# Activation-table choice, a residual added by matmul, and per-tile normalisation in a two-block transformer kernel

## Chip, cores and metric

The kernel runs on one core of one Trainium2 chip. The metric is device time of one launch in microseconds (us), the median of the runs shown. Everything is float32 at the interface; the input has 256 tokens of width 1024, handled as two tiles of 128 tokens.

## What is computed

The reference chains two blocks. Cut to what matters here:

```python
# first block: attention, then a mixture of 32 experts, top 4
h = layer_norm(DEEPNORM_ALPHA * x + moba_attention(x, ...), ln_g[0], ln_b[0])   # ALPHA = 2 ** 0.25
f = moe_ffn(h, ...)
x = layer_norm(DEEPNORM_ALPHA * h + f, ln_g[1], ln_b[1])

# second block
h = rmsnorm(x, pre_mix_g);  z = h @ w_in                 # 1024 -> 3584
mix = concat(hgrn2_mixer(z...), gate_b * causal_dwconv(gate_c * conv_h)) @ w_out
x = x + rmsnorm(mix, post_mix_g)
h = rmsnorm(x, pre_ffn_g);  u = causal_dwconv(h @ ffn_w_up)   # 1024 -> 2 * 2816
y = (silu(gate) * val) @ ffn_w_down
out = x + rmsnorm(y, post_ffn_g)
```

Each normalisation needs one 1/sqrt per token. The forget gate of `hgrn2_mixer` needs exp, log(1 + exp) and exp again.

## The kernel before

Five engine programs are written out by hand, tied by counting semaphores; there is no scheduler. Instructions of an engine run in the order of the source, and `link(...)` makes an engine wait for its own last instruction.

- **First block.** The attention projections, attention, the first layer norm (`layer_norm`, L1311, with `h1` as its result), the router. Then 32 experts in turn (L705 to L798): TensorE does `gather`, `gate_up` (L668), `down_e` (L676) and `scatter` (L688), which adds an expert's output into the PSUM banks 4 to 7. The banks begin with the gated down biases (L729, at expert 1). SyncE streams each expert's weights in six pieces of 2 MB through a ring of nine slots, each load waiting until the piece nine places back has been used.
- **Second layer norm (L1471).** For each tile of 128 tokens VectorE adds `ALPHA * h1` to the banks (L1317, two halves of 512), takes the moments (`bn_stats` L1320, `bn_aggr` L1322), and then in `scale` applies them in two passes over 1024 columns (L1327, L1328), giving `x2`.
- **Roots.** 1/sqrt is made in two steps. VectorE writes the variance plus epsilon (`root_of`, L1294). ScalarE makes a rough root as exp(-0.5 * ln v) (`rough_root`, L952 and L953). VectorE refines it by one Newton step of four tiny instructions (`refine`, L1301 to L1304). There are 13 such roots, six in the two layer norms and the norm before the first product, one for the heads, six later.
- **Before each product of the second block.** ScalarE squares a tile of tokens and sums it (L1086, L1173), a root is made, VectorE scales the tile into `xn` (L1477, L1621). TensorE transposes `xn` (`turn_tokens`, L806), all of it after both tiles are ready. ScalarE evicts each of the eight transposed chunks of 128 channels rounded to the high part `x_hi` (`evict_hi`, L975), VectorE the remainder `x_lo` (`evict_lo`, L1238). `product` (L532) multiplies one piece of 256 weight columns: for each half of it and each of eight chunks, three matmuls of 128x256 (hi*hi, lo*hi, hi*lo), 48 in all. It begins after all eight chunks of both parts.
- **Weight pieces.** `split_hi` (ScalarE, L968, 128x2048) and `split_lo` (VectorE, L1231) make the two parts of a weight piece in two alternating buffers. The split of a piece waits for the product two places before it.
- **Forget gate (L1091 to L1103, L1486 to L1513).** After products 0 and 1 ScalarE does Abs, Exp, Ln on each half, VectorE turns them into log f, runs two prefix sums (L1497, L1499), the first decays, and only then `split_lo` of piece 4.
- **Third and fourth junction.** After the output projection (`mix`, L883) the squares of `mix` for both tiles, then two roots, `rms_residual` for both tiles (L1604 to L1611, giving `x3`), the squares of `x3` for both, two roots, `xn`, and the product with `ffn_w_up` (`UP`, 22 pieces). After the down projection (L924) squares of both tiles, two roots, `rms_residual` into `y_out`, and one store per tile.

## Time and profile before

| | |
|---|---|
| time before, median of 3 runs | 1524.03 us (1523.1 to 1526.42) |
| the profiled execution's own time | 1528.25 us |
| its span, first to last instruction | 1526.3 us |
| mean granted TensorE clock | 0.954 of full |
| busy in the span: TensorE matmul | 1359.2 us (89%) |
| VectorE / ScalarE / GpSimd | 431.0 / 361.1 / 57.6 us |
| moved by DMA | 482.57 MB, mean 316 GB/s |

Busy time says how long an engine worked, not whether anybody waited for it. The stretches are: attention up to about 175 us; the experts up to about 1100 us, in which the DMA engines move some 430 GB/s; the second block's mixer up to 1291 us; its feed-forward part to the end. TensorE is busy nearly throughout, so its idle stretches are what the other engines add.

### The profile page before, as it was taken

The page shows a single profiled execution, that of the slowest core. Times are in us where ns is not written, and L with a number is a line of the kernel's source. Part 1 is how long each engine was busy: PE and PEld are TensorE (multiplying, and loading weights), DVE is VectorE, ACT ScalarE, POOL GpSimd, SP SyncE. Part 2 cuts the span into 40 slices and gives each one's busy share as a digit, 9 for nine tenths or more (in the row PEclk, how much of TensorE's full clock was granted, in tenths as well). Part 3 has the DMA queues.
Part 4 walks back from the last instruction along what each step waited for, and adds up shares of the span by engine and source line. Part 5 has one row for each costly group of instructions (what it writes and reads, how often), then busy time and mean ns, then how long its engine had stood idle before and what let it go on. Part 6 is the DMA issues. An engine that isn't in the chain of part 4 may idle for free.

```text
span 1526.3 us, 16757 instructions
## 1 busy us (share of the span) xinstructions
PE 1359.2 (89%) x7266; PEld 723.4 (47%) x7266; DVE 431.0 (28%) x722; ACT 361.1 (24%) x559; POOL 57.6 (4%) x72
## 2 busy tenths in 40 slices
PE   6988799999969999999999999999748877599995
PEld 6964433333323333333333233333248873599984
DVE  3421321011011101011010010011255661577754
ACT  3332101011001101011010011011255423666644
POOL 1001000000000000000000000000000000033300
PEclk9999699999989999999999999999969999699998
DMA  9661498999999999999999999999933412255420
GB/s 379 272 262 49 171 431 346 431 429 430 432 429 428 432 430 430 431 430 431 429 432 432 430 430 431 430 431 429 418 120 129 148 56 84 82 175 203 176 83 27
DMA packets 73864, 482.57 MB, mean 316 GB/s; under 512 B 4316, under 2 KB 26896, under 8 KB 49216
## 3 DMA queue, kind: packets, MB, share of 16 engines
q1 hardware_dynamic: 71824, 475.53, 75.0%
q0 software_dynamic: 1968, 5.97, 1.3%
q8 instruction: 58, 0.95, 0.2%
q14 instruction: 14, 0.11, 0.0%
HBM read 480.42 MB, written 1.06 MB: 315 GB/s over the span
## 4 chain that ended last, share of the span: by engine, by line
PE 67%; DMA 19%; DVE 7%; ACT 4%; issue 2%; POOL 0%; SPq 0%; ACTq 0%; DVEq 0%
PE bank L668 20%; PE bank L542 16%; DMA ring<-in_moe_w_gate_up 15%; PE bank L676 11%; PE bank L924 4%; PE bank L641 3%; PE bank L522 3%; PE bank L688 3%; DMA ring<-in_w_in 3%; PE bank L883 2%; PE bank L610 2%; PE bank L660 2%; ACT w_hi L968 1%; DMA arena<-rel_rows 1%; DVE w_lo L1231 1%
## 5 line engine op out<-in xcount | busy, mean ns | idle before, releaser
L668 PE MATMUL bank<-ring,arena 128*64 128x512 f32 x2048 | 451.6, 595 | 21.0 <-DMA ring<-in_moe_w_gate_up 21.0
L668 PEld LDWEIGHTS bank<-ring,arena 128*64 128x64 f32 x2048 | 142.2, 137 | 328.2 <-issue 282.7
L676 PE MATMUL bank<-ring,arena 128*64 128x512 f32 x1024 | 226.8, 595 | 0.9 <-ACT arena L1044 0.9
L1429 DVE TENSOR_SCALAR arena<-bank 128x512 f32<-128x512 f32 x32 | 22.1, 692 | 674.9 <-PE bank L668 674.8
L542 PE MATMUL bank<-x_hi,w_hi 128*128 128x256 f32 x640 | 185.4, 290 | 9.9 <-DVE w_lo L1231 6.0
L542 PE MATMUL bank<-x_lo,w_hi 128*128 128x256 f32 x640 | 184.2, 288 | 0.0
L542 PE MATMUL bank<-x_hi,w_lo 128*128 128x256 f32 x640 | 184.0, 288 | 0.0
L1231 DVE TENSOR_TENSOR w_lo<-ring,w_hi 128x2048 fp32r<-128x2048 f32 x59 | 135.1, 2292 | 133.8 <-ACT w_hi L968 133.8
L968 ACT CAST w_hi<-ring 128x2048 fp32r<-128x2048 f32 x59 | 112.2, 1905 | 175.2 <-PE bank L542 142.7
L1038 ACT ACTIVATE arena<-arena 128x512 f32<-128x512 f32 x32 | 20.2, 630 | 508.3 <-DVE arena L1429 508.3
L676 PEld LDWEIGHTS bank<-ring,arena 128*64 128x64 f32 x1024 | 70.7, 137 | 135.7 <-issue 127.9
L542 PEld LDWEIGHTS bank<-x_hi,w_hi 128*128 128x128 f32 x640 | 125.9, 197 | 11.0 <-issue 8.7
L522 PE MATMUL bank<-cst,arena 128*128 128x128 f32 (+1 forms) x412 | 67.2, 314 | 69.6 <-DVE arena L1621 22.6
L542 PEld LDWEIGHTS bank<-x_lo,w_hi 128*128 128x128 f32 x640 | 125.7, 196 | 0.0
L542 PEld LDWEIGHTS bank<-x_hi,w_lo 128*128 128x128 f32 x640 | 125.6, 196 | 0.0
L522 PEld LDWEIGHTS bank<-cst,arena 128*128 128x128 f32 (+1 forms) x412 | 54.9, 197 | 103.0 <-DVE arena L1437 28.0
L641 PE MATMUL bank<-arena 128*64 128x512 f32 x256 | 65.7, 637 | 11.5 <-issue 10.5
L688 PE MATMUL bank<-arena 64*128 64x512 f32 x256 | 64.5, 622 | 4.8 <-ACT arena L1054 4.8
L1054 ACT COPY arena<-bank 128x512 f32<-128x512 f32 x32 | 18.8, 586 | 199.6 <-PE bank L676 199.6
L1648 DVE SCALAR_TENSOR_TENSOR ring<-ring,vcol 128x256 f32<-128x256 f32 x88 | 48.8, 594 | 0.8
L688 PEld LDWEIGHTS bank<-arena 64*128 64x128 f32 x256 | 22.2, 188 | 46.7 <-issue 40.2
L641 PEld LDWEIGHTS bank<-arena 128*64 128x64 f32 x256 | 19.0, 144 | 50.8 <-issue 49.7
(244 smaller groups left out, 1121.6 us busy)
## 6 DMA issues: line engine op xcount, KB each, us to landing
ring<-in_moe_w_gate_up SPq DMA_DIRECT2D x128, 2048.0 KB, 24.1
ring<-in_moe_w_down SPq DMA_DIRECT2D x64, 2048.0 KB, 26.0
ring<-in_ffn_w_up SPq DMA_DIRECT2D x22, 1024.0 KB, 7.4
ring<-in_w_in SPq DMA_DIRECT2D x7, 2048.0 KB, 19.5
ring<-in_a_w_in SPq DMA_DIRECT2D x6, 2048.0 KB, 18.8
ring<-in_ffn_w_down SPq DMA_DIRECT2D x5, 2048.0 KB, 7.7
ring<-in_a_w_out SPq DMA_DIRECT2D x2, 2048.0 KB, 17.5
ring<-in_w_out SPq DMA_DIRECT2D x2, 2048.0 KB, 8.2
```

Source lines behind the costliest of these rows:

```text
L522: return pe.transpose(dst, src, ident[0:rows, 0:rows])
L542: last = mm(dst[:, j * T:(j + 1) * T], lhs, rhs, start=c == 0 and n == 0, stop=c == KC - 1 and n == 2)
L610: last = mm(bank[2 * g + t][:, :], oT[:, h, t * P:(t + 1) * P], slot(ATTN_OUT[g], KC)[:, h, :], start=h == 0, stop=h == H - 1)
L641: last = mm(bank[2][half * 64:half * 64 + 64, :], sel[:, t, :], h1[:, t, half * 512:(half + 1) * 512], start=t == 0, stop=t == NT - 1)
L660: mm(bank[q][half * 64:half * 64 + 64, :], bias_sel[rows, :], bgu[rows, half, :], start=True, stop=False)
L668: last = mm(bank[q // 2][half * 64:half * 64 + 64, :], chunk(xeT, c), w[:, c % 2, q * 512:(q + 1) * 512], start=False, stop=c == KC - 1)
L676: last = mm(bank[3][half * 64:half * 64 + 64, :], chunk(actT, c), w[:, c % 4, half * 512:(half + 1) * 512], start=c == 0, stop=c == KC - 1)
L688: last = mm(bank[4 + 2 * half + t][:, :], selgT[rows, t, :], y_item[rows, :], start=False, stop=True, skip_group_check=True)
L924: last = mm(bank[2 * t + g][:, :], a, w[:, cols], start=c == 0 and k == 0, stop=c == FB - 1 and k == 2)
L968: copy(like(w_hi, p), pieces[p][2]).then_inc(hi_ready, 1)
L1231: tt(like(w_lo, p), pieces[p][2], like(w_hi, p).bitcast(f32), ALU.subtract).then_inc(lo_ready, 1)
L1648: last = stt(y[:, g, :], u[:, g, j:j + T], vcol[:, col:col + 1], y[:, g, :], ALU.mult, ALU.add)
```

## The change

Line numbers of the changed file differ. The change does four things.

1. **One activation table.** Four places of ScalarE's program call for the table set that has both logarithm and exponential (at the start, after the experts, before the first `decay`, before the squares at the end), so that Ln and Exp alternate without a load between them.
2. **Second residual by TensorE.** At expert 24, after the scatter of expert 23, four matmuls of 128x512 add `ALPHA * I` times `h1` to the banks 4 to 7. VectorE makes `alpha_i` at expert 1. The second layer norm then reads the banks directly: `bn_stats` from PSUM, first pass of the scale from PSUM in two halves, no separate addition.
3. **Tile by tile.** At each of the three later junctions squares, root, scaling and the next squares are ordered for tile 0 first and then tile 1, and TensorE transposes tile 0 as soon as its `xn` is ready.
4. **Chunk by chunk.** The first product after a transposition (`IN2` piece 0, `UP` piece 0) waits before each chunk in its first half for that chunk alone.

```diff
+RESIDUAL_AT = 24
+        alpha_i = at(7168, P)
...
-            def product(p, dst, tokens_stationary=False):
+            def product(p, dst, tokens_stationary=False, fresh=0):
...
                     for c in range(KC):
+                        if fresh and j == 0:
+                            pe.wait_ge(hT_hi, fresh * KC - KC + c + 1)
+                            pe.wait_ge(hT_lo, fresh * KC - KC + c + 1)
...
+                if i == RESIDUAL_AT:
+
+                    pe.wait_ge(alpha_ready, 1)
+                    for g in range(2):
+                        for t in range(NT):
+                            mm(bank[4 + 2 * g + t][:, :], alpha_i, h1[:, t, g * 512:(g + 1) * 512], start=False, stop=True,
+                               skip_group_check=True)
...
             def turn_tokens(src, ready, ps):
 
-                for t in range(NT):
-                    pe.wait_ge(*ready(t))
+                def half(b, j, t):
+                    return turn(bank[b][:, j * T + t * P:j * T + (t + 1) * P],
+                                src[:, t, (2 * b + j) * P:(2 * b + j + 1) * P])
+
+                pe.wait_ge(*ready(0))
                 for b in range(4):
                     for j in range(2):
-                        for t in range(NT):
-                            last = turn(bank[b][:, j * T + t * P:j * T + (t + 1) * P],
-                                        src[:, t, (2 * b + j) * P:(2 * b + j + 1) * P])
-                    last.then_inc(ps, 1)
+                        half(b, j, 0)
+                pe.wait_ge(*ready(1))
+                for b in range(4):
+                    half(b, 0, 1)
+                    half(b, 1, 1).then_inc(ps, 1)
...
-            pe.wait_ge(hT_hi, KC)
-            pe.wait_ge(hT_lo, KC)
             for r in range(8):
-                for last in product(IN2 + r, bank[r], r >= 4):
+                if r < 4:
+                    pe.wait_ge(hT_lo, min(KC, 2 * r + 2))
+                for last in product(IN2 + r, bank[r], r >= 4, fresh=r == 0):
...
-            pe.wait_ge(x3_ready, NT)
...
-                for last in product(UP + f, bank[4 + f % 2]):
+                for last in product(UP + f, bank[4 + f % 2], fresh=2 * (f == 0)):
...
+            log_exp = "natural_log_exp_and_others"
+            nc.scalar.preload_act_table_set(log_exp)
...
+            nc.scalar.preload_act_table_set(log_exp)
             rough_root(2)
             rough_root(3)
             for t in range(NT):
                 act.wait_ge(x2_ready, t + 1)
                 activate(squares_at(t * D, D), x2[:, t, :], ACT.Square, accum_out=ss[:, t:t + 1]).then_inc(x_sq, 1)
-            rough_root(4)
-            rough_root(5)
+                rough_root(4 + t)
...
+            for t in range(NT):
+                act.wait_ge(mix_ps, 2 * t + 2)
+                squares_of(t, (2 + 2 * t, 3 + 2 * t), mix_sq)
+                rough_root(7 + 2 * t)
                 act.wait_ge(x3_ready, t + 1)
-                activate(squares_at(t * D, D), x3[:, t, :], ACT.Square, accum_out=ss2[:, 4 + t:5 + t]).then_inc(x_sq, 1)
-            rough_root(9)
-            rough_root(10)
+                activate(squares_at(2 * D + t * D, D), x3[:, t, :], ACT.Square, accum_out=ss2[:, 4 + t:5 + t]).then_inc(x_sq, 1)
+                rough_root(8 + 2 * t)
...
+            nc.scalar.preload_act_table_set(log_exp)
+            for t in range(NT):
+                act.wait_ge(down_ps, t + 1)
+                squares_of(t, (2 * t, 2 * t + 1), down_sq)
+                rough_root(11 + t)
...
+                    ts(alpha_i, ident, ALPHA, None, ALU.mult).then_inc(alpha_ready, 1)
...
-            layer_norm(x2, h1, bank[4:8], 2, lambda t: (moe_done, t + 1), x2_ready)
+            for t in range(NT):
+                dve.wait_ge(moe_done, t + 1)
+                for g in range(2):
+                    last = dve.bn_stats(stats[:, t, g, :], bank[4 + 2 * g + t][:, :])
+                link(last)
+                link(dve.bn_aggr(moments[:, t, :], stats[:, t, :, :].rearrange("p a b -> p (a b)")))
+                root_of(2 + t, moments[:, t, 1:2], 1.0, LN_EPS)
+            for t in range(NT):
+                r = refine(2 + t)
+                for g in range(2):
+                    cols = slice(g * 512, (g + 1) * 512)
+                    last = stt(x2[:, t, cols], bank[4 + 2 * g + t][:, :], moments[:, t, 0:1], row_g[:, cols],
+                               ALU.subtract, ALU.mult)
+                link(last)
+                if t:
+                    dve.wait_ge(x_sq, 1)
+                    root_of(4, ss[:, 0:1], 1.0 / D, RMS_EPS)
+                stt(x2[:, t, :], x2[:, t, :], r, row_b, ALU.mult, ALU.add).then_inc(x2_ready, 1)
+            for t in range(NT):
+                if t:
+                    dve.wait_ge(x_sq, 2)
+                    root_of(5, ss[:, 1:2], 1.0 / D, RMS_EPS)
+                r = refine(4 + t)
                 ts(xn[:, t, :], x2[:, t, :], r, None, ALU.mult).then_inc(xn_ready, 1)
```

**Order, place one.** ScalarE from the end of expert 31 to the first eviction of `x_hi`. Before (L1054 copies the last expert's output out of PSUM, L952/L953 are Ln/Exp of a root, L1086 the squares):

```order
269 L1054 COPY arena<-bank 128x512
270 L952 ACT_TABLE_LOAD
271 L952 ACTIVATE arena<-arena 128x1
272 L953 ACT_TABLE_LOAD
273 L953 ACTIVATE arena<-arena 128x1
...
278 L1086 ACTIVATE arena<-arena 128x1024 x2
279 L952 ACT_TABLE_LOAD
280 L952 ACTIVATE arena<-arena 128x1
281 L953 ACT_TABLE_LOAD
282 L953 ACTIVATE arena<-arena 128x1
```

And in the changed program (L1070 the copy, L968/L969 the root, L1103 the squares):

```order
265 L1070 COPY arena<-bank 128x512
266 L1098 ACT_TABLE_LOAD
267 L968 ACTIVATE arena<-arena 128x1
268 L969 ACTIVATE arena<-arena 128x1
269 L968 ACTIVATE arena<-arena 128x1
270 L969 ACTIVATE arena<-arena 128x1
271 L1103 ACTIVATE arena<-arena 128x1024
272 L968 ACTIVATE arena<-arena 128x1
273 L969 ACTIVATE arena<-arena 128x1
274 L1103 ACTIVATE arena<-arena 128x1024
```

One load stands where eight stood, and the first root of the norm has moved between the two squares. In the whole program of ScalarE there are 7 table loads where there were 35.

**Order, place two.** VectorE in the second layer norm, with what each row waits for. Before, tile 1's moments and the first scale:

```order
400 L1317 SCALAR_TENSOR_TENSOR arena<-arena,bank 128x512 [waits moe_done]
401 L1317 SCALAR_TENSOR_TENSOR arena<-arena,bank 128x512
402 L1320 BN_STATS arena<-arena 128x6 [waits dve_step]
403 L1320 BN_STATS arena<-arena 128x6
404 L1322 BN_AGGR arena<-arena 128x2 [waits dve_step]
...
410 L1327 SCALAR_TENSOR_TENSOR arena<-arena 128x1024 [waits dve_step]
411 L1328 SCALAR_TENSOR_TENSOR arena<-arena 128x1024 [waits dve_step]
```

In the changed program tile 1's moments and its scale:

```order
399 L1490 BN_STATS arena<-bank 128x6 [waits moe_done]
400 L1490 BN_STATS arena<-bank 128x6
401 L1492 BN_AGGR arena<-arena 128x2 [waits dve_step]
...
414 L1498 SCALAR_TENSOR_TENSOR arena<-bank,arena 128x512 [waits dve_step]
415 L1498 SCALAR_TENSOR_TENSOR arena<-bank,arena 128x512
416 L1309 TENSOR_SCALAR arena<-arena 128x1 [waits x_sq,dve_step]
417 L1504 SCALAR_TENSOR_TENSOR arena<-arena 128x1024
```

The addition is gone, the moments and the first pass read PSUM, and the variance of the next root (L1309, `root_of`) is written ahead of tile 1's last pass.

## Rows read from the trace of the kernel before

**Rows 1.** Waits of TensorE from 1120 to 1330 us: us in total, times, longest.
```profile
PE bank L522 <- DVE arena L1621: 22.6, 1, 22.6
PE bank L522 <- DVE arena L1477: 21.3, 1, 21.3
...
PE bank L542 <- DVE w_lo L1231: 4.6, 1, 4.6
```
**Rows 2.** Groups of instructions of ScalarE: count, busy us, mean ns, idle before.
```profile
L952 ACT ACT_TABLE_LOAD x13 | 16.7, 1283 | 0.2
```
**Rows 3.** Timeline of VectorE, 1102 to 1124 us: start, us, instruction, [idle before].
```profile
1102.96 1.28 DVE L1317 SCALAR_TENSOR_TENSOR arena<-arena,bank 128x512 f32<-128x512 f32 x2
1104.27 1.29 DVE L1320 BATCH_NORM_STATS2 arena<-arena 128x6 f32<-128x512 f32 x2
...
1109.61 1.28 DVE L1327 SCALAR_TENSOR_TENSOR arena<-arena 128x1024 f32<-128x1024 f32 x1
...
1119.75 0.16 DVE L1301 TENSOR_TENSOR arena<-arena 128x1 f32<-128x1 f32 x1 [4.18 <-ACT arena L953]
...
1123.12 0.16 DVE L1301 TENSOR_TENSOR arena<-arena 128x1 f32<-128x1 f32 x1 [1.78 <-ACT arena L953]
...
1123.90 0.75 DVE L1477 TENSOR_SCALAR arena<-arena 128x1024 f32<-128x1024 f32 x1
```
**Rows 4.** Timelines of ScalarE, VectorE and TensorE, 1124 to 1137 us.
```profile
1125.92 3.40 ACT L975 ACTIVATE x_hi<-bank,vcol 128x256 fp32r<-128x256 f32 x8 [2.83 <-PE bank L522]
...
1126.79 3.44 DVE L1238 SCALAR_TENSOR_TENSOR x_lo<-bank,vcol,x_hi 128x256 fp32r<-128x256 f32 x8 [2.14 <-ACT x_hi L975]
...
1124.80 3.65 PE L522 MATMUL bank<-cst,arena 128*128 128x128 f32 x16 [21.29 <-DVE arena L1477]
1130.33 0.55 PE L542 MATMUL bank<-x_hi,w_hi 128*128 128x256 f32 x1 [1.89 <-ACT x_hi L975]
...
1136.33 0.28 PE L542 MATMUL bank<-x_lo,w_hi 128*128 128x256 f32 x1
```
**Rows 5.** Timeline of VectorE, 1150 to 1161 us.
```profile
1151.06 0.69 DVE L1490 SCALAR_TENSOR_TENSOR arena<-bank,ring 128x512 f32<-128x512 f32 x1 [2.09 <-ACT ring L1098]
...
1158.38 2.29 DVE L1231 TENSOR_TENSOR w_lo<-ring,w_hi 128x2048 fp32r<-128x2048 f32 x1
```
**Rows 6.** Timelines of ScalarE and VectorE, 1295 to 1319 us.
```profile
1300.55 1.04 ACT L1173 ACTIVATE arena<-arena 128x1024 f32<-128x1024 f32 x1
1301.49 0.19 ACT L1173 ACTIVATION_READ_ACCUMULATOR arena<-arena 128x1 f32 x1
...
1295.19 0.16 DVE L1301 TENSOR_TENSOR arena<-arena 128x1 f32<-128x1 f32 x1 [9.48 <-ACT arena L953]
...
1295.97 1.41 DVE L1608 SCALAR_TENSOR_TENSOR arena<-bank,arena 128x512 f32<-128x512 f32 x2
1297.41 1.22 DVE L1611 TENSOR_TENSOR arena<-arena 128x1024 f32<-128x1024 f32 x1
...
1313.52 2.29 DVE L1231 TENSOR_TENSOR w_lo<-ring,w_hi 128x2048 fp32r<-128x2048 f32 x1 [0.26 <-ACT w_hi L968]
1315.73 3.22 DVE L1238 SCALAR_TENSOR_TENSOR x_lo<-bank,vcol,x_hi 128x256 fp32r<-128x256 f32 x8
```
**Rows 7.** Chain that ended last, in order of time: the whole product with `ffn_w_up`.
```profile
1319.05 128.44 PE bank L542 x1056
```
**Rows 8.** Timeline of VectorE from 1508 us to the end.
```profile
1514.34 0.16 DVE L1301 TENSOR_TENSOR arena<-arena 128x1 f32<-128x1 f32 x1 [5.34 <-ACT arena L953]
...
1522.04 1.23 DVE L1611 TENSOR_TENSOR arena<-arena 128x1024 f32<-128x1024 f32 x1
```
**Rows 9.** Page, costliest groups: `gate_up` of all experts, with its idle time and releaser.
```profile
L668 PE MATMUL bank<-ring,arena 128*64 128x512 f32 x2048 | 451.6, 595 | 21.0 <-DMA ring<-in_moe_w_gate_up 21.0
```
**Rows 10.** Timeline of TensorE, attention's output projection, 32 matmuls of 128x512.
```profile
122.94 27.73 PE L610 MATMUL bank<-ring,arena 128*128 128x512 f32 x64 [0.46 <-ACT arena L1016]
```
**Rows 11.** DMA issues: size and us from issue to landing.
```profile
ring<-in_moe_w_gate_up SPq DMA_DIRECT2D x128, 2048.0 KB, 24.1
```

More of the change, by code:

```diff
@@ L265, in build @@
         xe_ps, xe_ready, xeT_ps, xeT_ready = sem("xe_ps"), sem("xe_ready"), sem("xeT_ps"), sem("xeT_ready")
+        alpha_ready = sem("alpha_ready")
         sel_ready, selg_ready, bsel_ready = sem("sel_ready"), sem("selg_ready"), sem("bsel_ready")
@@ L1159, in _, with squares_of @@
                              scale=vcol[:, 160 + h:161 + h]).then_inc(mT_ready, 1)
-            def squares_of(ps, count, banks, done):
-                for n, b in enumerate(banks):
-                    if n % count == 0:
-                        act.wait_ge(ps[0], ps[1](n))
-                    last = activate(squares_at(n * 512, 512), bank[b][:, :], ACT.Square, accum_out=ss2[:, n:n + 1])
-                    last.then_inc(done, 1)
-            squares_of((mix_ps, lambda n: n + 2), 2, (2, 3, 4, 5), mix_sq)
-            rough_root(7)
-            rough_root(8)
+            def squares_of(t, banks, done):
+                for g, b in enumerate(banks):
+                    n = 2 * t + g
+                    activate(squares_at(n * 512, 512), bank[b][:, :], ACT.Square, accum_out=ss2[:, n:n + 1]).then_inc(done, 1)
             for t in range(NT):
+                act.wait_ge(mix_ps, 2 * t + 2)
+                squares_of(t, (2 + 2 * t, 3 + 2 * t), mix_sq)
+                rough_root(7 + 2 * t)
                 act.wait_ge(x3_ready, t + 1)
-                activate(squares_at(t * D, D), x3[:, t, :], ACT.Square, accum_out=ss2[:, 4 + t:5 + t]).then_inc(x_sq, 1)
-            rough_root(9)
-            rough_root(10)
+                activate(squares_at(2 * D + t * D, D), x3[:, t, :], ACT.Square, accum_out=ss2[:, 4 + t:5 + t]).then_inc(x_sq, 1)
+                rough_root(8 + 2 * t)
             split_hi(UP)
@@ L1214, in _ @@
                 split_a_hi(p)
-            act.wait_ge(down_ps, 1)
-            squares_of((down_ps, lambda n: n // 2 + 1), 2, (0, 1, 2, 3), down_sq)
-            rough_root(11)
-            rough_root(12)
+            nc.scalar.preload_act_table_set(log_exp)
+            for t in range(NT):
+                act.wait_ge(down_ps, t + 1)
+                squares_of(t, (2 * t, 2 * t + 1), down_sq)
+                rough_root(11 + t)
         @block.vector
@@ L1470, in _ @@
             dve.wait_ge(ln1_in, 32)
-            layer_norm(x2, h1, bank[4:8], 2, lambda t: (moe_done, t + 1), x2_ready)
             for t in range(NT):
-                dve.wait_ge(x_sq, t + 1)
-                r = root(4 + t, ss[:, t:t + 1], 1.0 / D, RMS_EPS)
+                dve.wait_ge(moe_done, t + 1)
[20 more added lines that the diff above has]
+                r = refine(4 + t)
                 ts(xn[:, t, :], x2[:, t, :], r, None, ALU.mult).then_inc(xn_ready, 1)
@@ L1615, in _ @@
                 dve.wait_ge(mix_sq, 2 * t + 2)
-                rms_residual(7 + t, t, (ss2[:, 2 * t:2 * t + 1], ss2[:, 2 * t + 1:2 * t + 2]), (2 + 2 * t, 3 + 2 * t), post_g, x2, x3,
-                             x3_ready)
-            for t in range(NT):
+                rms_residual(7 + 2 * t, t, (ss2[:, 2 * t:2 * t + 1], ss2[:, 2 * t + 1:2 * t + 2]), (2 + 2 * t, 3 + 2 * t), post_g,
+                             x2, x3, x3_ready)
                 dve.wait_ge(x_sq, NT + t + 1)
-                r = root(9 + t, ss2[:, 4 + t:5 + t], 1.0 / D, RMS_EPS)
+                r = root(8 + 2 * t, ss2[:, 4 + t:5 + t], 1.0 / D, RMS_EPS)
                 ts(xn[:, t, :], x3[:, t, :], r, None, ALU.mult).then_inc(xn_ready, 1)
```

2 lines of the change are left out of this document (removed).

## Prediction

> **What bounds the kernel now.** I read the page first, then the waits of TensorE, then the timelines at each wait. TensorE is busy for most of the span, and in the experts it waits for weights only. So time can be saved where TensorE stands still for other engines. Its waits in the second block [rows 1] name two such places: 21.3 us before the transposes of `x2` and 22.6 us before those of `x3`. A third, 4.6 us, is before weight piece 4. A fourth is no wait of TensorE: after its last matmul only squares, roots, `rms_residual` and stores are left [rows 8].
>
> What fills those waits is a chain between VectorE and ScalarE. A table load takes 1283 ns [rows 2]. The reader is to see in [rows 3] that VectorE idles 1.78 us for a rough root when one load lies between Ln and Exp. That idle time is 0.50 without it: 1.78 - 1.28. The refinement that follows takes 0.78 (1123.12 to 1123.90).
>
> **First junction, experts to product 0.** The sum starts at 1102.96, when VectorE takes up the norm; the weight splits ahead of it are not moved.
> - Norm before: from 1102.96 to 1109.61 it did two tiles' moments and one refinement. So a tile took (6.65 - 0.78) / 2 = 2.93, of which 1.31 is the addition (1102.96 to 1104.27) and 1.62 the moments. After: 2 x 1.62 gives 1106.2. The rough roots come 0.5 us after their variances and are hidden, since tile 1's moments lie between.
> - Scale of a tile after: 0.78, a first pass from PSUM in two halves, 1.44 as in [rows 6] (1295.97 to 1297.41), and a second of 1.28 [rows 3]. Tile 0 is ready at 1109.7, tile 1 at 1113.2. Tile 0's squares, root and Ln/Exp lie beside tile 1's passes.
> - `xn` of tile 0: 0.78 + 0.75, so 1114.7. Tile 1's squares (1.04 in the like row of [rows 6], about 1.2 with handing over) end at 1114.4, before that. Then epsilon 0.15, the 0.50, 0.78, 0.75: `xn` of tile 1 at about 1116.8. Before it was 1124.65. **7.9 us saved.**
> - Transposes: tile 0's eight take half of the 3.65 us [rows 4] and lie in the wait. Before, the first eviction began 1.12 us after the first transpose, after four of them; now two are needed, 0.46 us less. VectorE follows 0.87 us behind. Product 0 overwrites bank 0 and needs two chunks of `x_lo`, 2 x 0.43. So it starts 2.5 us after tile 1's transposes begin, where it took 5.53 (1124.80 to 1130.33). **3.0 us saved.** Later chunks come every 0.43 us, and three matmuls take 0.64 us at the low clock (28 starts from 1130.33 to 1136.33 are 0.214 each): no starving.
>
> **Forget gate.** Two loads on ScalarE lie between product 1 and the last Ln; VectorE takes it up at 1151.06 and, after prefix sums and decays, gets to the split of piece 4 at 1158.38 [rows 5]. TensorE waits 4.6 us for that split [rows 1], more than is saved: 2 x 1.28 = **2.6 us**. Next in line would be the end of product 3, 2 us further off. The load before the sigmoid stays.
>
> **Heads' root.** Its two loads go, but TensorE is in the 14 us of `mix` over the convolution half meanwhile: nothing.
>
> **Second junction, `mix` to `UP`.** Tile 0's rough root now comes before tile 1's squares: VectorE's idle 9.48 us [rows 6] shrinks to 0.50, so its refinement starts at 1286.2 instead of 1295.19. From there: 0.78 + 1.44 + 1.22 = 3.44 to `x3` of tile 0 at 1289.65; squares 1.2; epsilon and root 0.65; 0.78 and 0.75 for `xn`, 1293.0. Tile 1: adding two sums, epsilon and root 0.85, 3.44, squares 1.2, root 0.65: 1299.1. ScalarE's split of piece `UP` follows, 1.9 us, so VectorE's split starts at 1301.0 where it started at 1313.52. **12.5 us saved.** `x_lo` begins 2.21 after that as before, and the product needs one chunk, 0.43, instead of eight, 3.22: **2.8 us** more. Chunks come every 0.40 and three matmuls take 0.365 at the high clock (128.44 / 1056 = 0.122 each [rows 7]): 0.3 us lost. Together 15.0 us. The split of `UP + 1` ends some 6 us after the start, just in time.
>
> **End.** Tile 0's root no longer waits behind tile 1's squares and two loads: idle 5.34 [rows 8] becomes 0.50. Tile 1's idle 1.78 (the same 1.78 stands before four roots of a tile 1) becomes 0.50. The last addition at 1522.04 and the store follow. 4.84 + 1.28 = **6.1 us.**
>
> **Costs.** The four residual matmuls: the output projection did 32 of this shape in 27.73 us [rows 10], so 3.5 us. They are at expert 24, where TensorE waits for weights: it waits 21.0 us in all for them [rows 9], over the last dozen experts, and a load lands 24.1 us after issue though it moves 2 MB, under 5 us at 430 GB/s [rows 11]. So some four transfers are queued, and a place freed 3.5 us later starves nobody. I take 0, the bounds are 0 and 3.5. `alpha_i` on VectorE and the extra waits on ScalarE: 0, they lie beside `gate_up` of an expert.
>
> `bn_stats` from PSUM has no row. The nearest from below is 1.31 a pair from SBUF [rows 3]; from above, 1.44 for a pair that streams PSUM [rows 6]. I take the upper one: 2 x 0.13 = 0.25 us lost. The Trainium skill (Perfetto Trace Analysis, Optimizing Scalar/DVE Operations) gives VectorE an overhead of about 125 ns on PSUM against 60 on SBUF; by this, as an estimate, the four would lose 0.26.
>
> TensorE's clock: it fell during the idle wait and rose at 1136, 11 us after the first transpose, 6 after product 0 began [rows 4]. I assume the same, with 0.7 us lost because tile 0's transposes now stand apart. Bounds: no matmul at the low clock gains 28 x 0.092 = 2.6 at the first and about 1.5 at the second product, and both first products wholly at the low clock lose 5.
>
> **Sum.** 7.9 + 3.0 + 2.6 + 15.0 + 6.1 = 34.6, less 0.25 and 0.7: 33.7 us. The profiled execution took 1528.25 (span 1526.3), so its like would take 1494.6. It stands 4.2 above the median of the runs, 1524.03, from which I get **1490.3**. What a measurement of this kernel can tell from no change is about 0.2%, 3 us.
>
> **Rivals.**
> - *TensorE stays at 1.2 GHz after the split starts.* Transposes in two bursts and a product that waits chunk by chunk may not raise the clock. If it stays down for the first two products at both junctions, some 150 more matmuls cost 0.092: 14 us, so 1504. Against: at 1130.33 it began just as cold and was fast 6 us later [rows 4], and in the first junction the chunks come faster than it can use them. The Trainium skill (TensorE: Matmul & The Clock Gate, A second HAM failure mode: psum-queue depth-cycling) tells of short idling between groups of matmuls that makes the clock go up and down; by this rule it would come out as here, 1504. Chance 7%.
> - *The loads stay* or something else takes their time, that is, the change doesn't do what it says. Then each root on the path costs 1.3 to 2.6 more: 2.8 in the first junction, 6.5 in the second, 3.4 at the end, 2.6 in the forget gate, 15.3 in all. 1506. Against: the changed program has 7 loads, before 35. Chance 4%.
> - *The residual is paid:* the 3.5 us are on the path, 1494. For it: every expert after the pause waits for weights, so the stage ends with the DMA stream. Against: the queue depth above. Chance 5%.
> - *Slower than before.* If the clock fell at the new junction and did not come back within the `UP` product, all of its matmuls would pay 0.092. Beyond 33.7 / 0.092 = 366 of them, a third of the 1056, the gain is gone; all 1056 cost 97 us, so 1587. Against: within this product's 128.44 us there is hardly room for matmuls at 1.2 GHz. Chance 1%.
>
> **How the numbers follow.** My forecast has 83%. Its own range is from 34.6 + 4.1 saved, 1485, to the loss of 5 more on the clock and 3.5 for the residual, 1499. Two more for another chip and day: 1484 to 1500, which leaves out the rivals of 1504 and above. Faster 0.98, within 0.2% 0.01, slower 0.01.
>
> **What would show it.** Seven table loads. TensorE's wait before the first transposes of `x2` near 11 us with next to none before tile 1's; before those of `x3` near 2.3 us, and near 6 before tile 1's. No wait over 2.5 us for piece 4. VectorE idle 0.5 us before each refinement on the path. The tail from the last matmul to the last addition shorter by 6. Wrong: gate_up waits longer after expert 24; the first product's matmuls 0.21 us apart for much longer than 6 us; VectorE's idle before refinements still 1.8.

## The result and the profile after

The changed kernel takes **1487.31 us** (median, 1484.68 to 1490.52), the kernel before 1524.28 us (1523.1 to 1526.42) beside it. The ratio is 0.9757, 95% interval 0.9735 to 0.9779. Forecast were 1490.3 us and a range of 1484 to 1500. Measured once more later, both kernels anew, it was 1489.84 against 1523.86 us, ratio 0.9764 (0.9748 to 0.978). So 37.0 and 34.0 us were gained where 33.7 were forecast.

| | before | after |
|---|---|---|
| the profiled execution's own time, us | 1528.25 | 1487.63 |
| its span | 1526.3 | 1485.7 |
| mean granted TensorE clock | 0.954 | 0.966 |
| busy: TensorE matmul | 1359.2 | 1357.4 |
| VectorE / ScalarE / GpSimd | 431.0 / 361.1 / 57.6 | 428.5 / 324.3 / 57.9 |

The page of the changed kernel: busy time, then the group of `gate_up` (the line of [rows 9]).

```profile
PE 1357.4 (91%) x7274; PEld 720.5 (48%) x7274; DVE 428.5 (29%) x721; ACT 324.3 (22%) x531; POOL 57.9 (4%) x72
...
L674 PE MATMUL bank<-ring,arena 128*64 128x512 f32 x2048 | 451.1, 595 | 18.1 <-DMA ring<-in_moe_w_gate_up 18.0
```

TensorE is busy 1.8 us less, ScalarE 36.8 less. 28 loads of 1.283 us are 35.9, which is nearly all of the latter. The reader should not take 36.8 for the gain because it is near 37: many of those loads lay beside other work. What was gained shows in TensorE's waits.

Waits of TensorE in the changed kernel, 1060 to 1330 us (us in total, times, longest), the answer to [rows 1]:

```profile
PE bank L525 <- DVE arena L1510: 10.1, 1, 10.1
PE bank L525 <- DVE arena L1653: 8.2, 2, 6.0
...
PE bank L548 <- DVE w_lo L1246: 2.4, 1, 2.4
```

21.3 us became 10.1 (before `x2` is transposed), 22.6 became 8.2 in two pieces (before `x3` is), 4.6 became 2.4 (weight piece 4).

**First junction.** Timeline of VectorE, 1100 to 1114 us, the answer to [rows 3]:

```profile
1100.59 1.30 DVE L1490 BATCH_NORM_STATS2 arena<-bank 128x6 f32<-128x512 f32 x2
...
1103.88 0.15 DVE L1316 TENSOR_TENSOR arena<-arena 128x1 f32<-128x1 f32 x1
...
1104.64 1.41 DVE L1498 SCALAR_TENSOR_TENSOR arena<-bank,arena 128x512 f32<-128x512 f32 x2
...
1112.84 0.16 DVE L1316 TENSOR_TENSOR arena<-arena 128x1 f32<-128x1 f32 x1 [0.51 <-ACT arena L969]
...
1113.61 0.75 DVE L1510 TENSOR_SCALAR arena<-arena 128x1024 f32<-128x1024 f32 x1
```

Counted from the start of the norm, the first refinement comes after 3.29 us and `xn` of tile 1 is ready after 13.77 (1114.36 - 1100.59). Before it was ready after 21.69 (1124.65 - 1102.96). In the whole stretch VectorE idles once, 0.51 us for tile 1's rough root.

What follows on the three engines, the answer to [rows 4]:

```profile
1115.15 3.02 ACT L991 ACTIVATE x_hi<-bank,vcol 128x256 fp32r<-128x256 f32 x8 [2.34 <-PE bank L525]
...
1116.02 3.23 DVE L1253 SCALAR_TENSOR_TENSOR x_lo<-bank,vcol,x_hi 128x256 fp32r<-128x256 f32 x8 [1.65 <-ACT x_hi L991]
...
1112.33 4.07 PE L525 MATMUL bank<-cst,arena 128*128 128x128 f32 x16 [10.14 <-DVE arena L1510]
1116.95 0.58 PE L548 MATMUL bank<-x_hi,w_hi 128*128 128x256 f32 x1 [0.56 <-DVE x_lo L1253]
...
1120.53 0.39 PE L548 MATMUL bank<-x_lo,w_hi 128*128 128x256 f32 x1
...
1120.88 0.28 PE L548 MATMUL bank<-x_hi,w_hi 128*128 128x256 f32 x1
```

Product 0 starts at 1116.95, 0.93 us after the first `x_lo` begins: two chunks of it are done and six are still to come (the row of all eight lasts 3.23 us). It then never waits for a chunk. Its matmuls start 0.21 us apart until 1120.7 and 0.12 apart afterwards.

**Forget gate and piece 4.** Timeline of VectorE, the answer to [rows 5]:

```profile
1132.42 2.29 DVE L1246 TENSOR_TENSOR w_lo<-ring,w_hi 128x2048 fp32r<-128x2048 f32 x1 [2.08 <-ACT w_hi L984]
1134.63 0.68 DVE L1523 SCALAR_TENSOR_TENSOR arena<-bank,ring 128x512 f32<-128x512 f32 x1
...
1141.96 2.29 DVE L1246 TENSOR_TENSOR w_lo<-ring,w_hi 128x2048 fp32r<-128x2048 f32 x1
```

Before, L1490 (now L1523) had waited 2.09 us for the logarithm. Now it has no idle time at all in front: it follows the split of piece 3, which ends at 1134.7, 0.5 us after ScalarE's last Ln (1134.2).

**Second junction.** Timelines of VectorE and TensorE in the changed kernel, the answer to [rows 6]:

```profile
1267.08 0.16 DVE L1316 TENSOR_TENSOR arena<-arena 128x1 f32<-128x1 f32 x1 [0.50 <-ACT arena L969]
...
1280.00 0.16 DVE L1316 TENSOR_TENSOR arena<-arena 128x1 f32<-128x1 f32 x1 [0.50 <-ACT arena L969]
...
1281.79 2.29 DVE L1246 TENSOR_TENSOR w_lo<-ring,w_hi 128x2048 fp32r<-128x2048 f32 x1 [0.27 <-ACT w_hi L984]
...
1273.98 1.65 PE L525 MATMUL bank<-cst,arena 128*128 128x128 f32 x8 [2.29 <-DVE arena L1653]
1281.58 1.97 PE L525 MATMUL bank<-cst,arena 128*128 128x128 f32 x8 [5.95 <-DVE arena L1653]
1284.62 0.55 PE L548 MATMUL bank<-x_hi,w_hi 128*128 128x256 f32 x1 [1.07 <-ACT x_hi L991]
```

The 9.48 us of [rows 6] before tile 0's refinement are 0.50. All four refinements have 0.50 or 0.51 in front.

**End.** Timeline of VectorE, the answer to [rows 8]:

```profile
1475.01 0.16 DVE L1316 TENSOR_TENSOR arena<-arena 128x1 f32<-128x1 f32 x1 [0.50 <-ACT arena L969]
...
1481.43 1.23 DVE L1644 TENSOR_TENSOR arena<-arena 128x1024 f32<-128x1024 f32 x1
```

**Chain of waits** (start, us, what), the long products:

```profile
1116.95 13.46 PE bank L548 x96
...
1144.30 36.32 PE bank L548 x288
...
1284.62 128.45 PE bank L548 x1056
```

The last is 128.44 in [rows 7]: the `UP` product pays nothing for a start chunk by chunk.

### The span in stages

Spans differ by several us for reasons that are not the change, so from here on stages are compared. Each step is the us from one mark to the next; "x96" are products 0 and 1, "x288" products 4 to 9. All are read from one profile per kernel.

| step | before | again | after | again |
|---|---|---|---|---|
| norm of `x2` begins | 1102.96 | 1099.58 | 1100.59 | 1099.18 |
| to product 0 | 27.37 | 27.37 | 16.36 | 16.35 |
| to product 4 | 30.39 | 27.83 | 27.35 | 27.56 |
| of this, x96 | 14.33 | 11.77 | 13.46 | 13.68 |
| to `mix`, convolution half | 100.01 | 99.35 | 97.29 | 98.83 |
| of this, x288 | 37.52 | 36.84 | 36.32 | 36.32 |
| to `mix`, second half | 16.10 | 17.79 | 16.10 | 17.79 |
| to `UP` product | 42.22 | 42.22 | 26.93 | 26.93 |
| to down product | 136.24 | 137.23 | 136.24 | 136.43 |
| to the last squares | 54.72 | 54.72 | 54.72 | 54.72 |
| to the end | 16.29 | 16.31 | 10.12 | 10.11 |

Three steps repeat to 0.02 us in both profiles of either kernel: 27.37 to 16.36 (11.0), 42.22 to 26.93 (15.3), 16.30 to 10.12 (6.2). Those are the change's. Between products 0 and 4, without x96, 16.06 became 13.88 (2.2). x288 is 0.5 to 1.2 less. Together 35.2 to 35.9 us. The rest wanders by itself: x96 between 11.8 and 14.3, the second half of `mix` at 16.10 or 17.79, the time of the norm's start.

### The profile page after: what moved, and what is told of

It is laid out like the page before. It is cut to its first block, busy times and chain, and to the rows that moved or that the text cites. A ratio compares the mean times of both kernels' runs of the same rounds, so it can differ in the third digit from the quotient of the medians.

```text
span 1485.7 us, 16760 instructions
## 1 busy us (share of the span) xinstructions
PE 1357.4 (91%) x7274; PEld 720.5 (48%) x7274; DVE 428.5 (29%) x721; ACT 324.3 (22%) x531; POOL 57.9 (4%) x72
## 4 chain that ended last, share of the span: by engine, by line
PE 68%; DMA 19%; DVE 8%; ACT 2%; issue 2%; POOL 0%; SPq 0%; ACTq 0%; DVEq 0%
PE bank L674 21%; PE bank L548 16%; DMA ring<-in_moe_w_gate_up 15%; PE bank L682 11%; PE bank L937 3%; PE bank L647 3%; PE bank L694 3%; PE bank L525 3%; DMA ring<-in_w_in 3%; PE bank L616 2%; PE bank L666 2%; PE bank L899 1%; DVE w_lo L1246 1%; ACT w_hi L984 1%; DMA arena<-rel_rows 1%
## 5 line engine op out<-in xcount | busy, mean ns | idle before, releaser
L674 PE MATMUL bank<-ring,arena 128*64 128x512 f32 x2048 | 451.1, 595 | 18.1 <-DMA ring<-in_moe_w_gate_up 18.0
L1054 ACT ACTIVATE arena<-arena 128x512 f32<-128x512 f32 x32 | 20.2, 630 | 505.0 <-DVE arena L1445 505.0
L525 PE MATMUL bank<-cst,arena 128*128 128x128 f32 (+1 forms) x412 | 66.8, 311 | 44.4 <-DVE arena L1510 10.1
L647 PE MATMUL bank<-arena 128*64 128x512 f32 x256 | 65.7, 637 | 11.5 <-issue 10.5
L1070 ACT COPY arena<-bank 128x512 f32<-128x512 f32 x32 | 18.7, 585 | 199.6 <-PE bank L682 199.6
```

Source lines behind the costliest of these rows:

```text
L525: return pe.transpose(dst, src, ident[0:rows, 0:rows])
L647: last = mm(bank[2][half * 64:half * 64 + 64, :], sel[:, t, :], h1[:, t, half * 512:(half + 1) * 512], start=t == 0, stop=t == NT - 1)
L674: last = mm(bank[q // 2][half * 64:half * 64 + 64, :], chunk(xeT, c), w[:, c % 2, q * 512:(q + 1) * 512], start=False, stop=c == KC - 1)
```

## The experiments

Two explanations compete throughout: that the forecast's parts are right one by one, or that its sum is right by chance, with a part too large beside one too small. The runs undo or isolate one part each. Unless said otherwise a ratio is to the kernel before, and a diff is to the changed kernel.

### Both kernels again

> The kernel before, unchanged, for a second profile of it. In the first one the down-bias matmuls at expert 1 took 6.74 us and the norm started at 1103.0; in the changed kernel and all its variants they took 3.7 to 4.5 and it started at 1097 to 1101. If that is how TensorE's clock happened to stand, it differs here by 1 us or more; if the change caused it, both numbers come back. The two times differ by less than 2 us. After the 4.6 us wait for piece 4 the 288 matmuls take 37.5 us again, and not the 36.3 of the variants with the 2.4 us wait, if the length of a wait sets the clock behind it.

Measured: 1524.71 against 1523.86 us, ratio 1.0009 (1.0 to 1.0018). The second profile bears on the late start of the norm in the first profile of before. Chains of waits of the two executions of the same kernel, the gated down biases at expert 1, of the first:

```profile
224.32 6.74 PE bank L729 x8
```

and of the second, with its first long products:

```profile
224.35 4.09 PE bank L729 x8
...
1126.95 11.77 PE bank L542 x96
...
1154.78 36.84 PE bank L542 x288
```

The same eight matmuls, starting at the same time, took 6.74 or 4.09 us; from 224.3 to 231.1 the mean granted clock was 0.54 in the first execution and 0.75 in the second. So the 2.4 us by which the norm began earlier after the change are not the change's: the kernel before has its start at 1102.96 or 1099.58. One expectation was missed: x288 took 36.84 us and not 37.5 again, so its excess over the 36.3 behind the shorter wait is 0.5 to 1.2 us.

> The changed kernel, unchanged, for a second profile and a time on the same chip as the other two. The steps between marks of the program (norm to product 0 16.4, mix to UP 26.9, last squares to end 10.1) come back within 0.1; what differs lies in stretches where TensorE's clock moves.

Measured: 1489.84 us, ratio 0.9764 (0.9748 to 0.978). The stages are in the table above.

### The activation table alone

Diff to the kernel before, the added line at each of the four places:

```diff
+            nc.scalar.preload_act_table_set(log_exp)
```

> The kernel before with the table choice alone (four calls), everything else as before. Theory A (each load on a waiting path costs its 1.28 us and nothing else): 3.8 us before product 0, 2.2 at the forget gate (there VectorE's split of piece 3 takes over), 7.7 before UP, 3.8 at the end, together 17.5 us: about 1506.8. Rival B (the loads were mostly hidden and the reordering did the work): under 8 us, 1516 or more.

Measured: 1502.75 us, before 1524.95 beside it, ratio 0.9861 (0.9842 to 0.9881). That is 22.2 us. Waits of TensorE, 1060 to 1330 us:

```profile
PE bank L522 <- DVE arena L1483: 17.2, 1, 17.2
PE bank L522 <- DVE arena L1627: 14.6, 1, 14.6
...
PE bank L542 <- DVE w_lo L1237: 2.4, 1, 2.4
```

The wait for piece 4 is already down to 2.4: that part of the gain is the table's alone. Stages, against the second profile of before: 4.0 in the first junction (27.37 to 23.38), 2.2 to product 4 without x96, 0.6 in x288, 8.0 in the second junction (42.22 to 34.25), 4.0 at the end. Together 18.8, where 17.5 were expected; the other 3.4 us of the medians lie in no stage that repeats.

### All but the activation table

The line is taken out at all four places.

```diff
-            nc.scalar.preload_act_table_set(log_exp)
```

> The changed kernel without the four calls, so with 35 loads again. Theory A: roots cost 1.3 to 2.6 us more each on the path, 2.8 + 6.5 + 3.4, and 2.2 at the forget gate: 15 us above the changed kernel, about 1502. Rival B: within 5 us of the changed kernel. If the gain of the table alone and the loss without it differ by more than 3 us, the table and the reordering overlap.

Measured: 1510.26 us, ratio 0.9895 (0.9878 to 0.9911), a gain of 14.7. Without the table the change is worth 14.7, the table alone 22.2, together 36.9, where the whole gave 37.0. They add up. By stages the loads cost 3.1 in the first junction, 2.2 to product 4 without x96, 0.9 in x288, 8.75 in the second junction and 3.4 at the end: 18.3, near the 18.8 from the other side.

The second junction cost more than expected. ScalarE's timeline there, from the end of the squares of `x3`, tile 0, to the load before that root's Exp (L967 is Ln, L968 Exp):

```profile
1283.91 0.19 ACT L1185 ACTIVATION_READ_ACCUMULATOR arena<-arena 128x1 f32 x1
1284.11 1.28 ACT L967 ACT_TABLE_LOAD   x1
1285.40 0.20 ACT L967 ACTIVATE arena<-arena 128x1 f32<-128x1 f32 x1
1285.62 1.28 ACT L968 ACT_TABLE_LOAD   x1
```

The load for Ln starts when the squares have ended. VectorE needs some 0.2 us from there for the variance plus epsilon (0.5 after the squares of `mix`, where it first adds two sums), so only that much of the load is hidden. Of the 2.57 us of two loads 2.19 stand on the path of each root, the mean of the four (8.75 / 4). The forecast's rival "the loads stay" had 6.5 us for this stage.

### The residual on VectorE again

```diff
-                if i == RESIDUAL_AT:
+                if False:
...
+                    last = stt(x2[:, t, cols], h1[:, t, cols], ALPHA, bank[4 + 2 * g + t][:, :], ALU.mult, ALU.add)
...
-                    last = dve.bn_stats(stats[:, t, g, :], bank[4 + 2 * g + t][:, :])
+                    last = dve.bn_stats(stats[:, t, g, :], x2[:, t, g * 512:(g + 1) * 512])
```

> The changed kernel with the second residual added by VectorE as before and the norm's passes on SBUF; the tile order stays. Theory A: two additions of 1.31 us come back and two first passes shrink by 0.16: 2.3 us above the changed kernel, all of it between the start of the norm and product 0. Rival C (the matmuls at expert 24 delay the weight stream): it gains 3.5 there, so 1 us below the changed kernel or more, and the norm starts earlier.

Measured: 1492.37 us, ratio 0.9792 (0.9771 to 0.9813). The first junction is 18.72 instead of 16.36, so the residual on TensorE is worth 2.4 us there. The medians say 2.5 to 5, which the wandering of the other stages covers. Page of this kernel, `gate_up`:

```profile
L674 PE MATMUL bank<-ring,arena 128*64 128x512 f32 x2048 | 451.6, 595 | 20.8 <-DMA ring<-in_moe_w_gate_up 20.8
```

and the moments from SBUF in VectorE's timeline:

```profile
1100.57 1.29 DVE L1493 BATCH_NORM_STATS2 arena<-arena 128x6 f32<-128x512 f32 x2
```

This answers two costs at once. `gate_up` waits 20.8 us without the four matmuls and 18.1 with them: most of their 3.5 us displace a wait for weights. The norm starts at 1099.25 without them, and between 1097.11 and 1101.23 in the ten profiles with them. What stands in front of it in the chain of waits is a load of weights, after it their splits; here in the changed kernel:

```profile
1053.67 40.47 DMA ring<-in_w_in
```

And a pair of `bn_stats` takes 1.29 from SBUF, 1.30 from PSUM: the 0.25 us that I had taken for four are not there. The Trainium skill (Perfetto Trace Analysis, Optimizing Scalar/DVE Operations) has an overhead of about 125 ns on PSUM against 60 on SBUF; for this instruction the trace does not show it. The first pass of the scale is slower from PSUM, 1.41 for two halves against 1.28 for one whole pass from SBUF. Reading PSUM alone does not explain that: the addition of [rows 3] reads a bank too, as its second operand, and two halves of it take 1.28. What makes the difference was not isolated.

### The residual at expert 12

```diff
-RESIDUAL_AT = 24
+RESIDUAL_AT = 12
```

> The changed kernel with the four residual matmuls at expert 12, where TensorE does not wait for weights, instead of 24. If the weight stream sets the end of the experts, TensorE's 3.5 us at expert 12 are taken up by later waits for weights: 0 to 1 us, and the waits of gate_up shrink by about 3.5. If TensorE's own work sets it, 3.5 us above the changed kernel.

Measured: 1487.49 us, ratio 0.9768 (0.9749 to 0.9786): no difference. Page, `gate_up`:

```profile
L674 PE MATMUL bank<-ring,arena 128*64 128x512 f32 x2048 | 451.1, 595 | 18.2 <-DMA ring<-in_moe_w_gate_up 18.1
```

It waits as long as with the matmuls at expert 24. That they cost nothing is thus shown for both places. My reason for the place (they come when TensorE waits anyway) was not what mattered: it is enough that waits for weights still follow.

### No start chunk by chunk

```diff
+            pe.wait_ge(hT_hi, KC)
+            pe.wait_ge(hT_lo, KC)
             for r in range(8):
-                if r < 4:
-                    pe.wait_ge(hT_lo, min(KC, 2 * r + 2))
-                for last in product(IN2 + r, bank[r], r >= 4, fresh=r == 0):
+                for last in product(IN2 + r, bank[r], r >= 4):
```

and the same before the `UP` product.

> The changed kernel with both first products waiting for all eight chunks again. Theory A: six chunks of 0.40 to 0.43 us at the first, seven at the second less the 0.3 it was held up: 2.5 + 2.5, 5 us above the changed kernel. Rival D (a product that waits chunk by chunk runs longer on the low clock): only 2 to 3 us, since both products then run through faster once begun.

Measured: 1494.35 us, ratio 0.9801 (0.978 to 0.9821). First junction 18.75 (+2.4), second 29.62 (+2.7). The chain of waits at the first shows what comes back, eight evictions and a stretch in which nothing else is seen:

```profile
1112.39 3.04 ACT x_hi L993 x8
1115.43 1.16 issue
1116.58 14.05 PE bank L548 x96
```

The two steps are 5.1 us, expected were 5; medians differ by 7.0, or 4.5 against the later run of the changed kernel.

### Both tiles transposed together

```diff
-                pe.wait_ge(*ready(0))
+                for t in range(NT):
+                    pe.wait_ge(*ready(t))
                 for b in range(4):
                     for j in range(2):
-                        half(b, j, 0)
-                pe.wait_ge(*ready(1))
-                for b in range(4):
-                    half(b, 0, 1)
-                    half(b, 1, 1).then_inc(ps, 1)
+                        for t in range(NT):
+                            last = half(b, j, t)
+                    last.then_inc(ps, 1)
```

> The changed kernel with all transposes after both tiles, in the old order; chunks stay. Theory A: the first eviction waits for four transposes instead of two, 0.5 us at the first junction; nothing at the second, where VectorE's split of the weights is later. Together 0.5 us above. Theory E (the early burst of tile 0's transposes is what raised TensorE's clock earlier and gave the 3 us more than forecast): 2 to 4 us above, with a longer stretch at 1.2 GHz after the products start.

Measured: 1485.91 us, ratio 0.9742 (0.9726 to 0.9759). Nothing is lost, though the junctions grow by 0.9 and 0.7 us. The chain of waits at the first product,

```profile
1115.73 11.52 PE bank L548 x96
```

and at the `UP` product:

```profile
1283.62 127.78 PE bank L548 x1056
```

x96 is 11.52 where the changed kernel had 13.46, and x1056 is 0.67 less. 96 matmuls at 0.12 are 11.5, so product 0 began at the high clock, 2.4 GHz. Theory E, that tile 0's early burst raises the clock for the product, falls. That the two bursts lower it is not shown either: transposed apart, x96 was 11.79 and 11.80 in two of the other runs. One profile each cannot settle it, and it stays open whether the early transposes of tile 0 are worth anything.

### The old order of tiles from `mix` on

The squares of both tiles, then both roots, `rms_residual` of both, as before; likewise after the down projection.

```diff
             for t in range(NT):
                 act.wait_ge(mix_ps, 2 * t + 2)
                 squares_of(t, (2 + 2 * t, 3 + 2 * t), mix_sq)
-                rough_root(7 + 2 * t)
+            rough_root(7)
+            rough_root(8)
+            for t in range(NT):
                 act.wait_ge(x3_ready, t + 1)
```

> The changed kernel with squares and roots of the second junction and of the end in the order of before (both squares, both roots), table, residual and chunks as changed. Theory A: 4 us at the second junction and 2.3 at the end, 6 us above the changed kernel. Rival B (the reordering is the bulk): over 12 us.

Measured: 1493.63 us, ratio 0.9792 (0.9773 to 0.9812). Second junction 31.56 (+4.6), end 12.31 (+2.2); expected were 4 and 2.3. VectorE's timeline before the first refinement of `mix`:

```profile
1272.74 0.16 DVE L1320 TENSOR_TENSOR arena<-arena 128x1 f32<-128x1 f32 x1 [6.77 <-ACT arena L969]
```

6.77 us of idle time, where [rows 6] had 9.48 with the loads and the changed kernel has 0.50. So 2.71 of the 9.48 were loads, and 6.27 the order.

### A busy TensorE before the first product

Nine matmuls of 128x512 (two records each) whose result nobody uses are put ahead of the transposes of `x2`, where TensorE waits.

```diff
+            for _ in range(9):
+                mm(bank[0][:, :], ident, h1[:, 0, 0:512], start=True, stop=True)
             turn_tokens(xn, lambda t: (xn_ready, t + 1), hT_ps)
```

> The changed kernel with nine added matmuls of 128x512 (their result is not used) on TensorE right after the last scatter, in the 10.1 us in which it waits for xn of tile 0. If the low clock of product 0 comes from that wait, the clock is high when the transposes start: these take half as long and the first two products 11.5 to 12 us instead of 13.5, together 2 to 3 us below the changed kernel. If the added work overruns the wait or the clock falls anyway, 0 or above.

Measured: 1486.54 us, ratio 0.9768 (0.9751 to 0.9785). No gain can be told: 1487.49 us were measured beside it for the run with the residual at expert 12. Timeline of TensorE:

```profile
1100.95 8.69 PE L840 MATMUL bank<-arena,cst 128*128 128x512 f32 x18
1111.17 1.09 PE L525 MATMUL bank<-cst,arena 128*128 128x128 f32 x8 [1.53 <-DVE arena L1512]
1113.26 1.97 PE L525 MATMUL bank<-cst,arena 128*128 128x128 f32 x8 [1.00 <-DVE arena L1512]
```

and its windows (us, then busy us of TensorE, its weight loads, VectorE, ScalarE, GpSimd; granted clock; DMA share; GB/s):

```profile
1100.00:1110.00 10.00, 9.64 (x22) 3.69 (x18) 9.44 (x26) 2.65 (x9) 0.55 (x2) 0.88 0.99 387
1110.00:1117.00 7.00, 4.27 (x21) 3.63 (x22) 4.63 (x15) 4.29 (x12) 1.24 (x2) 0.69 0.68 266
```

Tile 0's eight transposes took 1.09 us, at a granted clock of 1.00; eight of the same shape take 1.65 in the changed kernel's second junction. But in the 7 us around the two bursts the mean clock was 0.69, tile 1's transposes took 1.97 again with the clock at 0.50, and x96 is 13.39 where it was 13.46. So in this execution the clock fell behind the filling, not in the long wait. TensorE was busy for 4.27 of the 7 us, 1.2 of them product 0 itself, with pauses of 1.53, 1.00 and 0.56. Neither the long wait nor the two short bursts decides alone how product 0 starts: in the runs with the residual at expert 12 and with the old order from `mix` on, the wait before the transposes is 10.6 and 10.5 us, the bursts stand apart in the same way, and product 0 begins at a clock of 1.00 (x96 11.79 and 11.80). What decides stays open.

### The split of piece 4 earlier

```diff
             link(dve.memset(marks[:, 64:HG * T:128], 1.0))
+            split_lo(IN2 + 4)
...
             decays(0)
-            split_lo(IN2 + 4)
```

That is ahead of the second prefix sum.

> The changed kernel with VectorE's split of piece 4 ahead of the second prefix sum, alone. TensorE's wait of 2.4 us goes. If it costs its length, products 0 to 9 take 2.4 us less than the changed kernel's 63.7; if it also pulls the clock down behind it, 4 us less, since all 288 matmuls behind it then run at the high clock. The time 2 to 4 us below the changed kernel.

Measured: 1485.36 us, ratio 0.9744 (0.9721 to 0.9766). The wait is gone, and products 0 to 9 are one piece of the chain:

```profile
1116.09 59.43 PE bank L548 x480
```

The changed kernel took 27.35 + 36.32 = 63.67 for them. A wait of 2.4 us was worth 4.2. Of the other 1.8 some 1.6 lie behind it: from the first to the last start of the 288 matmuls it is 36.02 us in the changed kernel and 34.44 here, and 34.44 again in the next run. Windows of 5.30 us right behind the wait, in the kernel before:

```profile
1160.70:1166.00 5.30, 5.28 (x24) 5.28 (x25) 3.37 (x3) 0.00 (x0) 0.00 (x0) 0.50 0.25 54
```

and in the changed kernel:

```profile
1144.30:1149.60 5.30, 5.30 (x32) 5.30 (x33) 3.34 (x3) 0.10 (x1) 0.00 (x0) 0.68 0.27 56
```

TensorE is full in both, yet does 24 matmuls behind the wait of 4.6 us, with the clock at 0.50 throughout, and 32 behind that of 2.4. In the second profile of before the clock came back earlier, with a mean of 0.57 over the same 5.30 us. That is the part of x288 that the change gained, and it repeats: x288 took 36.27 to 36.33 us in all nine profiles with the wait of 2.4, and 36.84, 37.19 and 37.52 in the three with that of 4.6.

### Splits earlier at both places

The same for piece 4, and the splits of pieces `UP` and `UP + 1` moved ahead of the squares of `mix`, on ScalarE and VectorE.

```diff
+            split_hi(UP)
+            split_hi(UP + 1)
             for t in range(NT):
                 act.wait_ge(mix_ps, 2 * t + 2)
                 squares_of(t, (2 + 2 * t, 3 + 2 * t), mix_sq)
```

> A version that may beat both: the changed kernel with the splits of UP pieces 0 and 1 moved ahead of the squares of mix (ScalarE and VectorE are idle during mix), and the split of piece 4 moved ahead of the second prefix sum. By the trace of the changed kernel the wait for piece 4 is 2.4 us and the first x_lo before UP waits 0.8 us for the split: 3 us below the changed kernel, about 1484. If another wait takes their place (the first decays come 2.3 us later), 0.8 or nothing.

Measured: **1483.68 us**, ratio 0.9721 (0.9701 to 0.9742), the fastest of all. Against the changed kernel it is 3.6 us by the medians; the intervals of the two ratios overlap a little, so the stages carry the claim. 59.49 for products 0 to 9 (the 4.2 of the run above), and the second junction is 26.10 instead of 26.93. At the second junction 0.8 were expected and 0.8 came, of 2.3 us of splits there (VectorE's 2.29 that ends at 1284.08 in the changed kernel): once the split is gone, the transposes and evictions are next.

## Why the prediction was right

Point by point, by its steps (us gained; measured is by stages):

| step | forecast | measured |
|---|---|---|
| first junction | 7.9 + 3.0 - 0.25 = 10.65 | 11.0 |
| forget gate | 2.6 | 2.2 |
| heads' root | 0 | 0 (16.10 or 17.79 in both kernels) |
| second junction | 12.5 + 2.8 - 0.3 = 15.0 | 15.3 |
| end | 6.1 | 6.2 |
| residual matmuls | 0 | 0 |
| clock | -0.7 | +0.5 to +1.2 |
| sum | 33.7 | 35.2 to 35.9 |

- **First junction.** The marks came where the text put them, counted from the norm's start: first refinement forecast at 3.24, measured 3.29; `x2` of tile 1 at 10.2, 10.24; `xn` of tile 1 at 13.8, 13.77; product 0 at 16.3, 16.36. Its parts, by the run that undoes each: 2.4 for the residual, 2.4 for the chunks, 3.1 for the loads, 0.9 for tile 0's early transposes. For the residual 2 x 1.31 stood in the sum, for the loads 2.8 in the rival. The remaining 2.3 us were not isolated; from the timeline I take them for tile 0's squares and root, which now lie beside tile 1's passes.
- **Forget gate.** The mechanism was right, the size 0.4 too large. Two loads of 1.28 were to be saved in full, with the end of product 3 named as next. Next was something nearer: VectorE's own split of piece 3, which now ends 0.5 us after the logarithm is ready. The run with the table alone gave the same 2.2.
- **Second junction.** Refinement to refinement, 12.9 us were forecast from tile 0's first to tile 1's last and 12.92 measured; the two waits were to be 2.3 and 6 and are 2.29 and 5.95. The idle 9.48 came out as forecast, and the run with the old order splits it into 6.27 and 2.71.
- **End.** 5.34 and 1.78 became 0.50 and 0.51, and the time is 6.2 less.
- **Costs.** The residual's matmuls cost nothing that can be seen, at expert 24 or 12, and `gate_up`'s wait fell by 2.6 to 3 with them. `bn_stats` from PSUM costs 0, not 0.25; I took the upper bound where the lower was the truth.
- **Clock: the step that was wrong, in size and in sign.** I looked for its cost only where new pauses come (the split bursts of transposes) and took 0.7. The gain is at a place that I had priced by its wait alone: behind the wait for piece 4, where x288 ran 0.5 to 1.2 us quicker once the wait had gone from 4.6 to 2.4. The prediction also has the clock fall during the idle wait before the transposes of `x2`. In the kernel before it was 1.00 until 1101, 0.76 from 1101 to 1103 while TensorE was busy with the last `scatter` (it had waited 4.1 us for that), and 0.50 from 1103 on, before the long wait had begun. In the first product x96 was 13.46 and 13.68, between the 11.77 and the 14.33 of the kernel before, so no change can be told there.

The sum did not come out by large errors that cancel: the forget gate was put 0.4 too high, and every other part at most 0.4 too low, but for the clock, which was 1.2 to 1.9 too low. That the median of the later pair, 34.0, lies so near to 33.7 is luck within the spread of the executions.

Of the rivals, the one on the clock that does not return gave 1504. It did not come: product 0 reached 2.4 GHz 3.8 us after its start, and x1056 took 128.45 and 128.65. The Trainium skill's rule beside it (TensorE: Matmul & The Clock Gate, A second HAM failure mode: psum-queue depth-cycling) would have given the same 1504; the trace shows a mean clock of 0.69 over two such bursts in one of the runs, but no loss in the products that follow beyond what the kernel before also has. The loads did not stay (7 are left); had they stayed, this rival's 15.3 would have been too little: 18.3 by stages, 20 to 23 by the medians. The paid residual is excluded by `gate_up`'s waits and the norm's starts in the runs with it at 24, at 12 and not at all. The slower case, with the clock down through the `UP` product, did not come.

The medians give 34.0 and 37.0 where the stages give 35.2 to 35.9. What is between, 1 to 2 us to either side, is as much as the steps that wander differ in two executions of one kernel; nothing more was shown of it.

## What to carry to other kernels

Price a chain between two engines mark by mark from rows of the same shape, and count every activation-table load that stands in it: here one choice of table gave over half of the gain, and the reordering of tiles, the residual and the chunks shared the rest. Where a reordering moves an engine's waits, price a wait of TensorE at more than its length. Before reading a difference of spans, take a second profile of each kernel and trust only the steps that repeat.

## What the runs showed of the hardware

- A wait of 2.4 us in a row of products cost 4.2: the granted clock behind it was 0.68 over 5.3 us, and 0.50 or 0.57 behind one of 4.6 us, with TensorE fully busy. The fall can come after the wait has ended: in the run without the start chunk by chunk the clock was 1.00 in the first microsecond behind the wait of 2.4, and 0.50 in the third and the fourth.
- Nine matmuls that kept TensorE busy for 8.69 us of a wait of 10 did not make the next two products faster in the execution profiled (13.39 us). With pauses of 1.53 and 1.00 us around the short bursts between, the clock was 0.69 again. Without them the same two products took 11.5 to 14.1 us in the other profiles with the changed order of the norm.
- The same eight matmuls of one kernel took 6.74 or 4.09 us in two executions, and a stretch of 16.10 us took 17.79 in others. Executions of one kernel spread over 3 to 10 us; between the two profiles of before, steps of this kind add up to all of the 3.9 us by which the spans differ.
- `bn_stats` over 512 columns takes as long from PSUM (1.30 the pair) as from SBUF (1.29).
